# One core, 35 stages of weight products: the order of the high and low products inside a unit

## What is computed

```python
u = hn @ e_w_in[j]                     # 2048 x 6144
mix = y @ e_w_out[j]                   # 2048 x 2048
h = h + jax.nn.sigmoid(h @ ple_gate_w[i]) * pl
u = hn @ o_w_in[j]                     # 2048 x 8208
h = rms_norm(x, norm_g) @ w_in         # second network, both layers
return x + (y @ w_out).astype(x.dtype)
```

## Time and profile before

| | |
|---|---|
| median of 3 runs | 2149.52 us |
| profiled execution, its own time | 2146.97 us |
| its span, from the first to the last instruction | 2145.2 us |
| mean granted clock of TensorE | 0.996 of full |
| busy: TensorE, weight loads, VectorE, ScalarE, GpSimd | 98%, 85%, 50%, 58%, 83% of the span |
| DMA | 378.77 MB, mean 177 GB/s |

### The profile page before, as it was taken

One profiled execution on the slowest core, in us unless ns is written; L12 is line 12 of the kernel. 1 busy time (PEld: TensorE's weight loads), 2 busy tenths in 40 slices (PEclk: granted clock), 3 DMA queues, 4 the chain that ended last, 5 costly groups with the idle time before them and its releaser, 6 DMA issues.

```text
span 2145.2 us, 37020 instructions
## 1 busy us (share of the span) xinstructions
PE 2097.2 (98%) x11876; PEld 1818.7 (85%) x11876; DVE 1074.3 (50%) x1863; ACT 1240.8 (58%) x2244; POOL 1780.8 (83%) x1421
## 2 busy tenths in 40 slices
PE   8999999999999999999999999999999999999997
PEld 7887888888888888888887888888888888888886
DVE  6556676245663246643466454414644651267612
ACT  6475456556555457765666465446655554476654
POOL 7799787999998887889998877897699889866696
PEclk9999999999999999999999999999999999999999
DMA  7565434566657555556566545664476666644464
GB/s 264 191 184 169 138 114 138 189 186 189 188 186 221 181 176 160 162 168 190 186 198 194 174 148 168 191 191 153 145 206 190 206 192 193 193 136 141 138 187 144
DMA packets 212259, 378.77 MB, mean 177 GB/s; under 512 B 23696, under 2 KB 36368, under 8 KB 211984
## 3 DMA queue, kind: packets, MB, share of 16 engines
q1 hardware_dynamic: 207936, 369.39, 56.0%
q10 hardware_dynamic: 4176, 7.53, 1.1%
HBM read 374.73 MB, written 2.10 MB: 176 GB/s over the span
## 4 chain that ended last, share of the span: by engine, by line
PE 75%; POOL 14%; issue 6%; DVE 4%; ACT 1%; POOLq 0%; DVEq 0%; ACTq 0%
PE ps L531 42%; PE ps L534 21%; POOL w_lo L452 13%; PE ps L518 2%; PE ps L519 2%; PE ps L520 2%; PE ps L762 2%; PE ps L789 1%; PE ps L634 1%; PE ps L774 1%; PE ps L589 0%; DVE ps L1511 0%; DVE tb L1510 0%; DVE sm L2234 0%; POOLq L451 0%
## 5 line engine op out<-in xcount | busy, mean ns | idle before, releaser
L452 POOL TENSOR_TENSOR w_lo<-raw,w_hi 128x512 fp32r<-128x512 f32 (+1 forms) x1406 | 1765.8, 1274 | 347.5 <-ACT w_hi L871 299.5
L871 ACT ACTIVATE w_hi<-raw 128x512 fp32r<-128x512 f32 (+2 forms) x1424 | 868.4, 618 | 747.1 <-PE ps L534 597.9
L531 PE MATMUL ps<-xa,w_hi 128*128 128x512 f32 x2592 | 824.9, 399 | 14.7 <-DVE xa L1566 8.6
L531 PE MATMUL ps<-xb,w_hi 128*128 128x512 f32 x2032 | 643.1, 397 | 2.1 <-POOL w_lo L452 2.1
L534 PEld LDWEIGHTS ps<-xa,w_lo 128*128 128x128 f32 x2592 | 488.0, 188 | 113.9
L534 PE MATMUL ps<-xa,w_lo 128*128 128x256 f32 x2592 | 513.2, 278 | 0.0
L534 PEld LDWEIGHTS ps<-xb,w_lo 128*128 128x128 f32 x2032 | 381.7, 188 | 89.5
L531 PEld LDWEIGHTS ps<-xa,w_hi 128*128 128x128 f32 x2592 | 398.2, 189 | 21.2 <-issue 11.7
L534 PE MATMUL ps<-xb,w_lo 128*128 128x256 f32 x2032 | 400.8, 278 | 0.0
L531 PEld LDWEIGHTS ps<-xb,w_hi 128*128 128x128 f32 x2032 | 312.4, 189 | 5.0 <-POOL w_lo L452 2.0
L1510 DVE TENSOR_SCALAR tb<-ps 128x512 f32<-128x512 f32 x99 | 67.8, 685 | 275.2 <-PE ps L534 274.6
(11 more groups left out here) (349 smaller groups left out, 2065.4 us busy)
## 6 DMA issues: line engine op xcount, KB each, us to landing
raw<-w_gate_dram SPq DMA_DIRECT2D x128, 256.0 KB, 3.0
raw<-w_ogz_dram SPq DMA_DIRECT2D x128, 256.0 KB, 3.0
raw<-w_ein_dram SPq DMA_DIRECT2D x96, 256.0 KB, 3.1
raw<-w_evout_dram SPq DMA_DIRECT2D x80, 256.0 KB, 2.9
raw<-w_odin_dram SPq DMA_DIRECT2D x80, 256.0 KB, 3.0
raw<-w_odgate_dram SPq DMA_DIRECT2D x72, 256.0 KB, 3.0
raw<-w_einz_dram SPq DMA_DIRECT2D x64, 256.0 KB, 2.9
raw<-w_eout_dram SPq DMA_DIRECT2D x64, 256.0 KB, 3.0
```

Of the source, the lines that this page charges most:

```text
L452: nc.gpsimd.tensor_tensor(w_lo[:, slot, 0:n], raw[:, at, 0:n], w_hi[:, slot, 0:n].bitcast(F32), SUB).then_inc(lo_pool, 1)
L531: mm(ps[:, bank + b, :], w_hi[:, slot, at], x[:, x0 + k, :], start=(k == 0), stop=False)
L871: af(w_hi[:, slot, 0:n], raw[:, at, 0:n], ACT.Copy).then_inc(act_rounded, 1)
```

## The change

In every stage with two output blocks, except the narrow and the `width` ones, the low product of a cell now follows its own high product: H0 L0 H1 L1 H2 L2 H3 L3. In ten stages the first unit of each pair has one of five other orders, from a table. The narrow stages get a loop of their own with the matmuls and the order that they had. The stages with `nb` = 1 keep their order too (it was H0 L0 H1 L1 already). The number of instructions, their operands, the waits and the counting of `unit_used` are unchanged.

```diff
+HIGH, LOW = 0, 1
+LEAD = {
+    "pairs": ((0, HIGH), (1, HIGH), (0, LOW), (1, LOW), (2, HIGH), (3, HIGH), (2, LOW), (3, LOW)),
+    "pair": ((0, HIGH), (1, HIGH), (0, LOW), (1, LOW), (2, HIGH), (2, LOW), (3, HIGH), (3, LOW)),
+    "inner": ((0, HIGH), (0, LOW), (1, HIGH), (2, HIGH), (1, LOW), (2, LOW), (3, HIGH), (3, LOW)),
+    "high": ((0, HIGH), (1, HIGH), (2, HIGH), (3, HIGH), (0, LOW), (1, LOW), (2, LOW), (3, LOW)),
+    "late": ((0, HIGH), (1, HIGH), (0, LOW), (2, HIGH), (1, LOW), (3, HIGH), (2, LOW), (3, LOW)),
+}
+LEAD_OF = {
+    "eout": "pairs", "gate0": "pair", "oqk": "inner", "ogz": "high", "oout": "late", "gate1": "inner",
+    "evmoba": "late", "evout": "pair", "odin": "pairs", "odout": "high",
+}
+
+
+def halves_in_turn(st, q):
+
+    if q == 0 and st.name in LEAD_OF:
+        return LEAD[LEAD_OF[st.name]]
+    return [(c, half) for c in range(len(st.units[q])) for half in (HIGH, LOW)]
...
-                    for c, (k, b) in enumerate(cells):
+                    for c, half in halves_in_turn(st, q):
+                        k, b = cells[c]
                         at = slice(c * P, c * P + P)
...
-                        mm(ps[:, bank + b, :], w_hi[:, slot, at], x[:, x0 + k, :], start=(k == 0), stop=False)
-                        for j in range(1 - st.nb, 1) if b == st.nb - 1 else ():
-                            lo_at = slice((c + j) * P, (c + j + 1) * P)
-                            ins = mm(ps[:, bank + b + j, 0:T], w_lo[:, slot, lo_at], x[:, x0 + k, 0:T],
+                        if half == HIGH:
+                            mm(ps[:, bank + b, :], w_hi[:, slot, at], x[:, x0 + k, :], start=(k == 0), stop=False)
+                        else:
+                            ins = mm(ps[:, bank + b, 0:T], w_lo[:, slot, at], x[:, x0 + k, 0:T],
                                      start=False, stop=(k == st.blocks - 1))
```

More of the change, by code:

```diff
@@ L522, in product @@
                         continue
-                    for c, (k, b) in enumerate(cells):
-                        at = slice(c * P, c * P + P)
[L525 to L530, removed]
-                        mm(ps[:, bank + b, :], w_hi[:, slot, at], x[:, x0 + k, :], start=(k == 0), stop=False)
-                        for j in range(1 - st.nb, 1) if b == st.nb - 1 else ():
-                            lo_at = slice((c + j) * P, (c + j + 1) * P)
-                            ins = mm(ps[:, bank + b + j, 0:T], w_lo[:, slot, lo_at], x[:, x0 + k, 0:T],
+                    if st.narrow:
+                        to = one_bank(st, p)
+                        for c, (k, b) in enumerate(cells):
+                            at = slice(c * P, c * P + P)
+                            mm(to[:, b, :], w_hi[:, slot, at], x[:, x0 + k, 0:T], start=(k == 0), stop=False)
+                            mm(to[:, b, :], w_hi[:, slot, at], x[:, x0 + k, T:2 * T], start=False, stop=False)
+                            ins = mm(to[:, b, :], w_lo[:, slot, at], x[:, x0 + k, 0:T], start=False,
+                                     stop=(k == st.blocks - 1))
+                        ins.then_inc(unit_used, 1)
+                        continue
+                    for c, half in halves_in_turn(st, q):
+                        k, b = cells[c]
+                        at = slice(c * P, c * P + P)
+                        if half == HIGH:
+                            mm(ps[:, bank + b, :], w_hi[:, slot, at], x[:, x0 + k, :], start=(k == 0), stop=False)
+                        else:
+                            ins = mm(ps[:, bank + b, 0:T], w_lo[:, slot, at], x[:, x0 + k, 0:T],
                                      start=False, stop=(k == st.blocks - 1))
```

## The result

The changed kernel takes 2155.84 us (median of 9 runs, 2153.64 to 2162.86), the one before 2149.05 us in the same runs (9 runs, 2147.62 to 2151.08): 1.0034 times as long, 95% interval 1.0025 to 1.0043. That is +6.8 us, slower as forecast, but a third of the forecast 19.6 us. The profiled execution took 2153.64 us, and its span is 6.6 us longer than before, so it has the whole of the loss in it.

What follows compares the result with a forecast made beforehand. TensorE was taken as the bound: 21.3 us for touched cells plus 0.3 for first units, less 2 hidden, gave +19.6 us on the median 2149.52, forecast 2169.1 us; 8-in-10 range 2150 to 2175.

Steps and rivals of the forecast that it cites:

- What bounds the kernel: Whole kernel: TensorE, busy 98% of the span, sets the time; a cell's cost is paid almost in full by the end.
- What hides it: TensorE's waits, mainly for GpSimd: 2 us of the 21.6 us added work taken as hidden, bounds 0 to nearly 11.
- The price of the new order: Touched two-bank stages: 353.3 ns per cell, as in `ogate` and `evkpe`, against 348.3; 5.0 ns x 4264 cells = 21.3 us.
- Bank and moving block: Output bank and activation block changes were held not to be the price, since single-size streams are cheapest; no separate size.
- The change of size: Switching between 512 and 256 columns was taken as the price: 346 ns without alternation, 348.3 two and two, 353.3 alternating.
- The counting of changes for the first units: Ten stages' first units: 10 ns per high-to-low change, giving +10 ns for 48 units, -10 for 24; together +0.3 us.
- Half of it: Rival, touched cells: price part size, part bank, the bank part saved; 2.5 ns per cell, about 2159 us; chance 0.15.
- Dearer: Rival, touched cells: bank and size changing at the same matmul cost +7.5 ns, 32 us, giving 2180 us; chance 0.05.
- The formula that I took from the Trainium skill: Matmul distance N / 2.4 + 2.5 ns whatever stands around it: 325 ns per cell in either order, change worth nothing.
- The lower edge of -2 ns: Lower bound on the touched cells' price: 346 ns without any mixing price against 348.3 in the old order.
- The prediction's own tests: Signs in the changed trace: 353 ns per cell in `oqk`, `oout`, `odin`; GpSimd waits under 7.9 us; `ogate`, `evkpe` as before.

Runs made afterwards that it cites:

- the first units alone: Changed kernel with its table of other first units kept, but the old order H0 H1 L0 L1 in all other two-bank units: 2148.54 us, one run.
- plain kernel: Changed kernel without its table of other first units, H L in turn in every two-bank unit: 2158.88 us, 1.0043 against the kernel before.
- the flip: Plain kernel with the first unit of pair 4 reordered in three stages (`oout` late, `gate1` and `evout` pair): 2157.53 us, one run.
- kernel with runs of four: Changed kernel with H0 H1 H2 H3 L0 L1 L2 L3 in every unit, one-bank stages H0 H1 L0 L1: 2157.18 us, 1.0037 against the kernel before.

## Why the prediction was right and where it failed

- **What bounds the kernel: right.** TensorE's price per cell comes out in the end time nearly in full; 7.8 us in the units, 6.6 in the span, 6.8 in the medians.
- **What hides it: wrong, and small.** I took 2 us as hidden in the waits for GpSimd; they went from 7.9 to 8.0 us, and all of TensorE's idle time shrank by 0.7. Here the waits didn't shrink because the streams before them were slower, they moved.
- **The price of the new order: the step that failed.** "I take the 5.0 ns for every touched cell." Measured: +5.0 ns where the stream is in course B and -1.6 where it is in A, nearly half of the units each. The mean is 7.8 us / 4624 = 1.7 ns. The rows were read rightly; `ogate` and `evkpe` gave the same 353 ns because both streams were in B, and I took two equal readings for proof of one price. They weren't independent: both stages come behind the old order, and in both traces with the old order (before, the first units alone) all three one-bank stages begin in B. Where the stage ahead of them alternates too, they begin in the course in which it ended, in all traces. No undisturbed stretch of the trace before is in A, so reading more of it wouldn't have shown this. `ogate` at 346.7 ns in the plain kernel shows that 353 was no price of the order. So does `evkpe` at 346.7 in the changed kernel, where I had expected it as before. The regular pattern of distances in `ogate` before, repeated every three cells, was the sign of a locked course, and I used it only to exclude waits.
- **Bank and moving block are not the price: right,** shown by `ogate` in both orders.
- **The change of size is: wrong.** The single-size streams (226 + 120 = 346 ns) set the floor, and course A reaches it while alternating at every matmul. The orders with the fewest changes are dearer than the old one. The counting of changes for the first units (+10 and -10 ns) goes with it; their sum of 0.3 us was right by luck: late cost about 1407 ns, pair 1407 or, where it led back to A, 1390, high 1388 in most and inner 1390 to 1396.
- **Of the rivals** none named this. "Half of it" has nearly its size (2159 us), by a mechanism (the bank) that the runs refute. "Dearer" has a slip: halfway from 353.3 to the dearest cell, 360, is +8.4 ns, not +7.5. The formula that I took from the Trainium skill (TensorE: Matmul & The Clock Gate, section Back-to-back issue gap) is given there for an isolated matmul, and I used it for a stream; it gives 216 ns for 512 columns where the single-size stream shows 226, and it knows of no two rates. The lower edge of -2 ns, "no price of mixing", was in the bounds, and it is what A costs.
- **The prediction's own tests** were the right place to look, but they asked for one number per stage. It was wrong to expect the same of `oqk`, `oout` and `odin`: 89.79, 89.21 and 112.99 us against 89.36, 89.26 and 111.67.

What stays open is what the state is, physically, and what in the orders "late" and "pair" moves it. That it is entered anew behind waits and other matmuls, kept otherwise, and moved by the order within one unit is shown; the flip itself was run once, but `gate0` and `evout` of the changed kernel show such moves too.

## What to carry to other kernels

A dense stream of matmuls of unequal size can have more than one steady rate, with the same instructions; a rate read from one stretch, or from two that happen to agree, is not the price of the order. Look for it in all stretches of the form and in more than one execution, and see whether a stretch after a stall returns to the same rate. Where several orders are free, the one with a single rate (here H H L L) is the safe choice, above all in streams that are broken up. The other is worth it only where something holds it in the cheap course.

## What the runs showed of the hardware

- Alternating matmuls of 512 and 256 columns, each with its own weight load, ran at 346.7 or 353.3 ns per pair at the full granted clock, and a stage of 64 units kept either from end to end (88.9 or 90.5 us).
- Two and two ran at 348.3 ns (two banks, in all traces that have it) and at 348 (one bank, in the kernel with runs of four); four and four at 351, eight and eight at 349 ns, though the same sizes in unmixed streams cost 226 and 120.
- The time at TensorE's lower clock (1.2 GHz, the higher level being 2.4) was 28.1 us in one execution of the plain kernel and 14.7 in the other. Some 11 us of it lay at the end of the kernel in both; the rest came behind waits of 1 to 2.8 us, and in the second execution most of these waits were not followed by a fall of the clock.
